# A decoder layer on one core: the last part of each head's triangular inverse, and what stands around it on the other engines, put in another order

## The reference

```python
h = rmsnorm(x, g_pre_mix);  proj = h @ w_in      # q|k|v, beta, decay, z, GLU input, gates a and b
qkv = silu(causal_dwconv(qkv_ext, conv_qkv_w))   # width 4
q, k = l2norm(q) * HEAD_K ** -0.5, l2norm(k)
# the delta rule in chunks of 64 tokens, per head:
lhs = strict_lower(beta * (k @ k.T) * decay) + eye
vw, kd = solve_triangular(lhs, [beta * v | beta * exp(gam) * k])
u = vw - kd @ s;  o = qd @ s + (qk * decay) @ u;  s = gl * s + ko.T @ u
o_a = rmsnorm(o) * silu(z)
c = causal_dwconv(glu, conf_dw_w) + conf_dw_b    # width 31, then over the channels:
o_b = silu(layernorm(c, conf_ln_g, conf_ln_b))
x = x + rmsnorm((sigmoid(gate_a) * o_a + sigmoid(gate_b) * o_b) @ w_out, g_post_mix)
y = x + rmsnorm(relu(rmsnorm(x, g_pre_ffn) @ w_up) ** 2 @ w_down, g_post_ffn)
```

## Time and profile before

| | us |
|---|---|
| time, median of 3 (lowest to highest) | 1051.16 (1051.08 to 1052.3) |
| the profiled execution's own time | 1051.12 |
| its span in the trace | 1049.3 |
| PE busy | 1031.2 |
| DVE busy | 739.0 |
| POOL busy | 647.9 |
| ACT busy | 595.3 |

### The profile page before, as it was taken

One profiled execution on the slowest core, in us unless ns is written; L12 is line 12 of the kernel. 1 busy time (PEld: TensorE's weight loads), 2 busy tenths in 40 slices (PEclk: granted clock), 3 DMA queues, 4 the chain that ended last, 5 costly groups with the idle time before them and its releaser, 6 DMA issues.

```text
span 1049.3 us, 21800 instructions
## 1 busy us (share of the span) xinstructions
PE 1031.2 (98%) x7929; PEld 1001.8 (95%) x7929; DVE 739.0 (70%) x1240; ACT 595.3 (57%) x1100; POOL 647.9 (62%) x568
## 2 busy tenths in 40 slices
PE   8999999999999999999999999999999999999997
PEld 6999899999999999999999999999999999999997
DVE  7989898898888988889767757594444444444335
ACT  7865646575565655656747855765444343343632
POOL 1895777785877858677684433647555555555631
PEclk9999999999999999999999999999999999999999
DMA  6322312223132231323221162123322233222302
GB/s 240 114 70 82 108 42 92 95 80 104 43 95 93 96 90 40 94 93 111 96 79 43 54 241 82 41 81 101 101 81 82 81 94 107 80 80 80 119 6 88
DMA packets 33883, 94.36 MB, mean 90 GB/s; under 512 B 4864, under 2 KB 12576, under 8 KB 33824
## 3 DMA queue, kind: packets, MB, share of 16 engines
q1 hardware_dynamic: 33824, 93.57, 27.3%
HBM read 85.02 MB, written 8.53 MB: 89 GB/s over the span
## 4 chain that ended last, share of the span: by engine, by line
PE 81%; DVE 6%; issue 4%; POOL 3%; ACT 3%; DVEq 0%; ACTq 0%; POOLq 0%
PE ps L784 26%; PE ps L1214 15%; PE ps L1162 13%; PE ps L793 7%; PE ps L1246 5%; PE ps L749 3%; DVE ps L1964 2%; DVE t_r L1961 1%; PE ps L936 1%; POOL in_lo L2659 1%; DVE work L2195 1%; PE ps L803 1%; POOL o_a L2659 1%; DVE work L2092 1%; POOL work L2659 1%
## 5 line engine op out<-in xcount | busy, mean ns | idle before, releaser
L2659 POOL TENSOR_TENSOR w_lo<-raw,w_hi 128x1024 fp32r<-128x1024 f32 x100 | 240.8, 2409 | 149.5 <-ACT w_hi L1790 50.2
L784 PE MATMUL ps<-in_hi,w_hi 128*128 128x288 f32 x944 | 285.9, 303 | 1.2 <-ACT work L1447 0.7
L784 PE MATMUL ps<-in_lo,w_hi 128*128 128x288 f32 x944 | 281.8, 300 | 0.7 <-POOL in_lo L2659 0.7
L784 PE MATMUL ps<-in_hi,w_lo 128*128 128x288 f32 x944 | 282.0, 299 | 0.0
L1964 DVE SCALAR_TENSOR_TENSOR ps<-work,ct,ps 128x512 f32<-128x512 f32 x240 | 180.7, 753 | 7.9 <-DVE work L2124 1.6
L784 PEld LDWEIGHTS ps<-in_hi,w_hi 128*128 128x128 f32 x944 | 177.6, 188 | 3.9 <-issue 2.4
L784 PEld LDWEIGHTS ps<-in_hi,w_lo 128*128 128x128 f32 x944 | 177.6, 188 | 0.7 <-issue 0.2
L784 PEld LDWEIGHTS ps<-in_lo,w_hi 128*128 128x128 f32 x944 | 177.2, 188 | 1.0 <-POOL in_lo L2659 0.9
L1961 DVE TENSOR_TENSOR o_a<-o_a,ps 128x576 f32<-128x576 f32 (+1 forms) x63 | 42.8, 682 | 107.6 <-PE ps L1214 73.3
L2659 POOL TENSOR_TENSOR w_lo<-t_pair,w_hi 128x1024 fp32r<-128x1024 f32 x18 | 43.6, 2423 | 42.5 <-ACT w_hi L1819 29.7
L2659 POOL TENSOR_TENSOR work<-work 128x576 f32<-128x576 f32 (+4 forms) x51 | 57.9, 1148 | 15.1 <-PE ps L1049 10.8
(11 more groups left out here) (408 smaller groups left out, 2816.7 us busy)
## 6 DMA issues: line engine op xcount, KB each, us to landing
raw<-w_all_in SPq DMA_DIRECT2D x135, 512.0 KB, 3.7
work<-s_in_in SPq DMA_DIRECT2D x8, 512.0 KB, 3.3
s_sample_out<-work SPq DMA_DIRECT2D x8, 512.0 KB, 4.4
xt<-x_t_in SPq DMA_DIRECT2D x4, 576.0 KB, 6.6
xt<-x_t_in SPq DMA_DIRECT2D x2, 1152.0 KB, 7.2
work<-decay_rows SPq DMA_DIRECT2D x7, 288.0 KB
y_out<-o_a SPq DMA_DIRECT2D x14, 144.0 KB, 1.8
halo<-halos_in SPq DMA_DIRECT2D x9, 156.0 KB, 3.6
```

Source lines behind the costliest of these rows:

```text
L784: t = mm(dense_ps(n, j, h), a[:, w, k], b[:, k, h * HALF:(h + 1) * HALF], start=r == 0, stop=r == PASS_MM // 2 - 1)
L2659: return gp.tensor_tensor(out, a, b, op)
```

## The change

It has seven parts, none of which changes what is computed.

1. `MIDDLE_AT`: of the eleven projection matmuls of slot 19 one goes to slot 20 (10 and 9 instead of 11 and 8). It stands behind lines 982 and 999.
2. ACT, passes 1 to 7: the table with the sigmoid is loaded at s=16, ahead of level six's copies; the read of CB's first half goes behind `x_r` and `u_r` of level seven.
3. `um`: POOL makes three quarters of it at s=16 instead of all of it at s=19 (two instructions, 64x4x64 and 128x4x64), waiting for T one level less far; the quarter that level seven completes is copied by ACT at the head of s=19 (64x4x64). `tmi_ready` now counts two per pass. `channel_sum` and CB's second read stand behind that copy on ACT.
4. DVE: the fourth tap and the reduce of v's short convolution go from ahead of `x_last` to behind it, ahead of `u_all`.
5. `early_3`: in pass 3 three of the 31-tap convolution's taps go from slots 8 and 12 to slots 2 and 3, and one more to slot 18.
6. Pass 1: `channel_sum(1)` goes behind the copy of the second chunk's u, in the same slot 24.
7. Last pass: from s=17 on DVE does T's steps ahead of the LayerNorm's. The last pair add and the three sums of pairs go from s=19 to s=20, behind `x_last` and ahead of `u_all`. ACT's squares of s=18 go behind `x_r` and `u_r`.

The diff, cut to what these parts touch:

```diff
-MIDDLE_AT = (12, 12, 14, 14, 14, 14, 12, 13, 12, 10, 10, 12, 10, 13, 11, 13, 12, 11, 11, 11, 8, 8,
+MIDDLE_AT = (12, 12, 14, 14, 14, 14, 12, 13, 12, 10, 10, 12, 10, 13, 11, 13, 12, 11, 11, 10, 9, 8,
...
+                for s in range(33):
+                    if s == 19:
+                        act.wait_ge(t_ready, LEVELS * n)
+                        A(quad(v["um"], 1, 0), quad(t_r, 1, 0).bitcast(F32), ACT.Copy).then_inc(tmi_ready, 1)
+                    if last(n) or s != 18:
+                        read_first(s)
...
                     casts(n, s)
+                    if not last(n) and s == 16:
+                        act.preload_act_table_set("sigmoid_and_others")
...
+                    if not n_is(n, 1) and s == (11 if last(n) else 19):
+                        channel_sum(n)
...
+                    if last(n) and 15 <= s < 18:
+                        mean_squares(s)
...
+                    if s == 18 and not last(n):
+                        read_first(s)
+                    if last(n) and s == 18:
+                        mean_squares(s)
...
                     if s in (22, 24, 26, 28):
                         chunk_u(n, (s - 22) // 2)
+                    if n_is(n, 1) and s == 24:
+                        channel_sum(n)
...
-            early_3 = {1: 4, 2: 1, 3: 2, 8: 2, 12: 1, 14: 1, 16: 1}
+            early_3 = {1: 4, 2: 2, 3: 3, 14: 1, 16: 1, 18: 1}
...
-                halves = (4, 7, 10, 12, 18, 19)
+                parts = {4: (0, 0, 2), 7: (0, 2, 4), 10: (1, 0, 2), 12: (1, 2, 4), 18: (2, 0, 2), 19: (2, 2, 3), 20: (2, 3, 4)}
...
+            def layer_norm(s):
+                if 14 <= s < 18:
+                    ...
+                        tt(two(conf[:, k]), two(conf[:, k]), job_ps(1), ALU.subtract).then_inc(xc_ready, 1)
+                if s in (16, 17, 18, 20):
+                    k = 6 if s == 20 else 2 * s - 32
+                    dve.wait_ge(xc_sq, k + 2)
+                    tt(xc_squares(k), xc_squares(k), xc_squares(k + 1), ALU.add).then_inc(xc_pair, 1)
...
+                    if last(n) and s < 17:
+                        layer_norm(s)
                     head(n, s)
+                    if last(n) and s >= 17:
+                        layer_norm(s)
...
-                    if last(n) and s == 19:
+                    if last(n) and s == 20:
                         for i, (a, b) in enumerate(((0, 2), (4, 6), (0, 4))):
...
+                    if s == 16:
+                        pool.wait_ge(t_ready, LEVELS * n - 1)
+                        pool.wait_ge(conv31_s, 2 * n)
+                        for a in range(2):
+                            rows, columns = (slice(0, HP), slice(0, P))[a], slice(a * HP, a * HP + HP)
+                            tt(pr(v["um"])[rows, :, columns], pr(t_r.bitcast(F32))[rows, :, columns],
+                               con("ident")[rows, columns].unsqueeze(1).to_broadcast([HP + a * HP, TILES, HP]), ALU.subtract)
+                        gp.tensor_copy(sample_half(0), by_sample(v["qn"][:, SEQ:TOK])).then_inc(tmi_ready, 1)
...
-                    if s == 19:
-                        pool.wait_ge(t_ready, LEVELS * n)
-                        pool.wait_ge(conv31_s, 2 * n)
-                        tt(pr(v["um"]), pr(t_r.bitcast(F32)), bc(con("ident")), ALU.subtract)
-                        gp.tensor_copy(sample_half(0), by_sample(v["qn"][:, SEQ:TOK])).then_inc(tmi_ready, 1)
```

More of the change, by code:

```diff
@@ L1479, in v_tile, with channel_sum @@
                 A(v["vts"][0:SMP], g(3)[0:SMP, 0:P], ACT.Copy).then_inc(vt_ready, 1)
+            def channel_sum(n):
+                act.wait_ge(conv31_done, n)
+                dst = conf[:, n - 1] if isinstance(n, int) else \
+                    conf[:, bass.ds(n - 1, 1)].rearrange("p a b -> p (a b)")
+                A(dst[:, 0:SEQ], acc31(), ACT.Identity, bias=ct[:, CF_TAPS:CF_TAPS + 1])
+                A(dst[:, SEQ:TOK], v["c31"][:, SEQ:TOK], ACT.Identity,
+                  bias=ct[:, CF_TAPS:CF_TAPS + 1]).then_inc(conf_ready, 1)
+                if not last(n):
+                    act.wait_ge(conf_ready, n)
+                    act.wait_ge(taps_cur, 2 * n + 1)
+                    A(ct[:], tap_of(n)[:, 3 * QK_TAPS:TAPW], ACT.Copy).then_inc(taps_cur, 1)
             def samples_u(n):
@@ L1486, in phase, with mean_squares, read_first @@
             def phase(n):
-                for s in range(33):
+                def mean_squares(s):
+                    for k in (2 * s - 30, 2 * s - 29):
+                        act.wait_ge(xc_ready, k + 1)
+                        A(xc_squares(k), conf[:, k], ACT.Square).then_inc(xc_sq, 1)
+                def read_first(s):
                     pos, j = evac_first(n, s)
@@ L2273, in convolutions @@
                     dve.wait_ge(gext_ready, n + 1)
[L2274 to L2277 removed]
+                parts = {4: (0, 0, 2), 7: (0, 2, 4), 10: (1, 0, 2), 12: (1, 2, 4), 18: (2, 0, 2), 19: (2, 2, 3), 20: (2, 3, 4)}
+                if proj and s in parts:
+                    qkv_conv(n, *parts[s])
                 if proj and s == 20:
@@ L2292, in head_cols @@
                 ve.tensor_copy(hc[:].unsqueeze(2), src).then_inc(hc_ready, 1)
+            def layer_norm(s):
+                if 14 <= s < 18:
+                    for k in (2 * s - 28, 2 * s - 27):
+                        if k == 0:
+                            dve.wait_ge(mu_ready, 1)
+                        tt(two(conf[:, k]), two(conf[:, k]), job_ps(1), ALU.subtract).then_inc(xc_ready, 1)
[3 more added lines that the diff above has]
+                    tt(xc_squares(k), xc_squares(k), xc_squares(k + 1), ALU.add).then_inc(xc_pair, 1)
             def phase(n):
                 for s in range(32):
[L2296 to L2304, removed]
                     if last(n) and 22 <= s < 26:
```

19 lines of the change are left out of this document (2 added, 17 removed).

## The result

| | before | changed |
|---|---|---|
| median of 20 executions (lowest to highest), us | 1051.17 (1050.16 to 1052.91) | 1053.11 (1051.37 to 1054.93) |
| ratio of the times, 95% interval | | 1.0016 (1.001 to 1.0023) |
| profiled execution, us, and span | 1051.12, 1049.3 | 1051.42, 1049.6 |

The change made the kernel slower, by 1.7 us going by the ratio and by 1.9 going by the medians, where 1.1 less was forecast and 1051.8 was the end of the range. That is little, under 0.2%, but the interval lies clear of 1. Two things have to be told apart. The profiled execution is only 0.3 longer than the one of before. But it is one of the fastest of its kernel: it and four others of the 20 had a clock figure (the granted TensorE clock, averaged over the execution) of 1.000 and took 1051.4 to 1051.9; the other 15 had 0.996 to 0.998 and took 1052.6 to 1054.9.

What follows compares the result with a forecast made beforehand. PE bounds it, busy 1031.2 of 1049.3 us, so only its waits count. Passes 4 to 7 -1.07, pass 3 -0.86, pass 2 -0.38, pass 1 0, last +1.22: -1.09 from 1051.12, so 1050.0; range 1047.3 to 1051.8.

Steps and rivals of the forecast that it cites:

- Passes 4 to 7, -1.07: PE's gap ahead of level seven's second product: 0.27 a pass saved, a gap of 0.17 staying, -1.07 in four passes.
- 0.1 in hand with the wake: Passes 4 to 7, line 1005: `u_all` ends about 361.83, PE wants it at 362.06; no gain and no cost.
- up to 0.1: Table load of 1.28 in 1.24 idle ahead of `uc_r`: if level six's product lacked slack, this much of 0.27 would go.
- CB's read, 0.02 ahead of job Z: Passes 4 to 7: CB's first read ends about 357.06, job Z's first matmul is reached at 357.08; called the tightest place.
- Pass 3, -0.86: Gaps at lines 964 and 984 go, -0.59, plus level seven's 0.27; bounds -0.27 to -1.03.
- Pass 2, -0.38: Line 997's wait for `x_last` goes, since a tap of 0.74 leaves from ahead of `x_last`: -0.38.
- Pass 1, 0: Line 1047's wait of 0.76 goes, but PE then waits at line 903 for an unchanged chain: 0.
- The last pass, +1.22: Level seven's 1.37 gap goes, but POOL's `w_lo` holds the first add and line 803 waits: +1.22; range end +0.07.
- The one in which the middle passes give nothing: Rival, 12%: CB's read or the table load late, passes 4 to 7 and part of pass 3 give 0: 1051.4.
- The slower one (the gate's chain): Rival, 9%: ACT's T quarter delays CB's second read, POOL's gate multiplies and DVE; 1.0 in passes 2 to 7: 1056.0.
- pass 1 gives its wait back: Rival, 9%: line 1047's visible wait in pass 1 is really saved, -0.93: 1049.1.

Runs made afterwards that it cites:

- part 7 alone: The kernel before with only the last pass's reordering (LayerNorm behind T's steps, four adds behind `x_last`): median 1053.12 us, ratio 1.0019 (1.001 to 1.0028).

## Why the prediction was wrong, step by step

- *Passes 4 to 7, -1.07.* The gap at level seven shrank as worked out. But two margins on which the prediction relied were not there. "0.1 in hand with the wake" for `u_all` was wrong: the working let `u_all` start as soon as the reduce had ended, and it started 0.30 later. The trace of before couldn't show this, since `u_all` waited for PE there, 0.43 from the reduce's end. PE was 0.09 late, and its first matmul behind the wait took 0.1 more. And the load at level six, which was put at nothing, cost the "up to 0.1" that the text allowed for. The 0.27 a pass was lost whole; with both mended the passes are 0.28 shorter. Parts 1 and 2 weren't tested one without the other.
- *CB's read, 0.02 ahead of job Z.* No wait showed there. The tightest place in the working was not the one that broke.
- *Pass 3, -0.86:* -0.73, since it too loses at line 1005. *Pass 2, -0.38:* -0.36, and line 997's gap is what went. *Pass 1, 0:* its length is equal with part 6 and without. Pass 3 was near, the other two right.
- *The last pass, +1.22:* +1.34 to line 803. The held add was right in kind and size: 2.01 instead of 0.75, and 0.62 behind POOL's end. Taking POOL's instruction away shows the cause (2.88 for four adds). The Trainium skill ("SBUF — State Buffer", "SBUF: two separate sides") has the instruction that starts first keep the shared port pair to its end. This case agrees where POOL's record opened 1.0 ahead of the first add, and POOL's instruction held it. It doesn't agree by the records where they opened 0.3 apart: POOL's subtraction opened at 557.75, ahead of the adds of 558.04, and yet it was the one that took 3.33, as in the earlier trace rows. Whether the pair is taken later than a record on POOL opens isn't shown.
- *The clock* is the step that failed and that took the time out of the range; without it the kernel stands at 1051.4, inside the range, with the gain gone in passes 4 to 7. The prediction worked out that PE would stand 2.6 us at line 803 and priced it at those 2.6 us alone; the fall of the clock behind it was put at nothing. In the trace that caught it, it took 1.6 more, and 25 of 31 executions have the low figure, against 24 of 106 of the kernel before. Undoing part 7 or shortening the stand to 1.42 takes the excess away, and part 7 alone brings it. The three executions of before that were at hand, 1051.08 to 1052.3, could have warned that single executions of one kernel lie 1.2 apart, but no trace on record showed a fall behind a stand.
- *The rivals.* The one in which the middle passes give nothing comes close to the profiled execution, 1051.42 where it said 1051.4. The size is in part luck: it let pass 3 lose 0.27, which lost 0.13, and the last pass cost 0.12 more than it said. The table load that it named had a part in it; but CB's read, its other cause, had none, and `u_all` had most. The slower one (the gate's chain) didn't occur: PE has no wait in slot 26. What forecast 1049.1 for "pass 1 gives its wait back" is refuted, since the old place of the channel sum gives the same pass.

Summed: in the profiled execution -1.09 was forecast and +0.3 came. Of the 1.4 between them 1.2 is passes 4 to 7, and the rest is the smaller gain in pass 3 and the dearer stand. The median lies 1.7 above the profiled execution, and there the clock is the cause as far as the traces go.

## What to carry to other kernels

An edit that turns several short waits of TensorE into one long one isn't neutral even if the sum is the same: price a stand of some 2 us (here 1.96 and 2.67) with the fall of the clock that can follow it, 1.6 us here, and look at how the granted clock and the time vary over the executions, since one profiled execution may show none of it. Before work is moved behind an instruction, see how much of it fits into the idle time ahead of that instruction; here three adds and a tap fitted ahead of `x_last` in idle time that the trace shows as "<-PE". An elementwise instruction with two operands in SBUF on DVE is to be kept out of the time of POOL's 2.4 us instructions where it is waited for, and a wait put on POOL is enough for that.

## What was not expected of the hardware

- The clock fell in one trace and not in the other of the same kernel, behind the same stand of 2.67 us. When it fell, 1.6 us were lost. Once it fell behind a stand of 1.59, at the kernel's end. Figures of 0.995 to 0.997, in the changed kernel 2.7 to 4.3 us above its fastest execution, were not caught in a trace; whether those have two falls stays open. The figure alone doesn't tell the loss: the kernel before has executions of 0.996 at 1051.58 and 1051.89 and one of 0.998 at 1053.01.
- A wait of DVE for its own reduce's result took 0.30 from the end of the one instruction to the start of the next (0.23 in pass 3).
- The group of line 1005 lasts 1.16 when PE has waited for it by 0.09, and 1.05 when it has not. The 0.1 lies between its first and its second matmul (0.21 apart, the others 0.11).
